# A 1-core, two-block network: the attention scores of the first block computed in two row groups at once

## The reference, cut to what matters

```python
# differential attention, 4 heads, two score maps c of 32 columns each
s = jnp.einsum('bqhcd,bkhcd->bhcqk', qi, k) * scale
p = jax.nn.softmax(jnp.where(causal, s, NEG_INF), axis=-1)
a = p[:, :, 0] - lam * p[:, :, 1]
# forgetting attention, 4 heads of 64 columns, cum = running sum of log forget gates
s = jnp.einsum('bqhd,bkhd->bhqk', qi, k) * scale
s = s + ci[..., None] - cum_k[:, :, None, :]
p = jax.nn.softmax(jnp.where(causal, s, NEG_INF), axis=-1)
```

## Time and profile before

| what | us |
|---|---|
| median of 3 runs | 2278.82 |
| lowest, highest | 2277.07, 2280.07 |
| profiled execution: its own time | 2276.64 |
| its span (first to last instruction) | 2274.9 |
| PE busy | 2214.5 (97%) |
| DVE busy | 1584.6 (70%) |
| mean granted TensorE clock | 0.983 |

### The profile page before, as it was taken

The page is one execution under the profiler, slowest core; times in us unless marked ns, Lnnn a source line. Parts: engine busy times, 40 slices in busy tenths (PEclk is TensorE's granted clock), DMA queues, the critical chain, the costliest instruction groups (busy, mean ns, idle before and its releaser), DMA issues.

```text
span 2274.9 us, 31866 instructions
## 1 busy us (share of the span) xinstructions
PE 2214.5 (97%) x11823; PEld 1866.6 (82%) x11833; DVE 1584.6 (70%) x1890; ACT 1096.2 (48%) x1288; POOL 51.3 (2%) x90
## 2 busy tenths in 40 slices
PE   7999999999999999999999999999999999999998
PEld 6887887887787887888788799978878879998887
DVE  6886877886777688666655778665566557867555
ACT  4434555434444455444544465654454446565443
POOL 1000010000000001000000000000000000000000
PEclk8999999999999999999999999999999999999999
DMA  8986555985687456666555463465556555435653
GB/s 309 348 307 208 166 170 181 343 308 187 235 293 242 144 167 204 216 220 210 176 194 183 153 183 112 149 198 184 190 167 203 185 185 150 141 114 173 201 186 109
DMA packets 325042, 454.56 MB, mean 200 GB/s; under 512 B 32722, under 2 KB 270040, under 8 KB 324952
## 3 DMA queue, kind: packets, MB, share of 16 engines
q1 hardware_dynamic: 320952, 440.98, 58.8%
q0 software_dynamic: 3728, 11.31, 1.7%
q10 hardware_dynamic: 272, 1.05, 0.1%
HBM read 449.91 MB, written 1.05 MB: 198 GB/s over the span
## 4 chain that ended last, share of the span: by engine, by line
PE 89%; DVE 6%; ACT 3%; issue 1%; DMA 1%; SPq 1%; DVEq 0%; ACTq 0%
PE ps L616 20%; PE ps L618 20%; PE ps L617 20%; PE ps L609 5%; PE ps L610 5%; PE ps L611 5%; PE ps L779 2%; PE ps L928 1%; DVE wlo L1952 1%; PE ps L761 1%; PE ps L762 1%; PE ps L764 1%; ACT whi L1329 1%; PE ps L706 1%; PE ps L727 1%
## 5 line engine op out<-in xcount | busy, mean ns | idle before, releaser
L1952 DVE TENSOR_TENSOR wlo<-raw,whi 128x2048 fp32r<-128x2048 f32 x348 | 791.5, 2278 | 364.8 <-ACT whi L1329 363.6
L1329 ACT ACTIVATE whi<-raw 128x2048 fp32r<-128x2048 f32 x346 | 659.8, 1910 | 271.4 <-PE ps L618 238.6
L616 PE MATMUL ps<-whi,xl 128*128 128x512 f32 x1472 | 591.5, 402 | 0.0
L618 PE MATMUL ps<-whi,xh 128*128 128x512 f32 x1472 | 574.2, 390 | 0.0
L617 PE MATMUL ps<-wlo,xh 128*128 128x512 f32 x1472 | 573.9, 390 | 0.0
L616 PEld LDWEIGHTS ps<-whi,xl 128*128 128x128 f32 x1472 | 276.5, 188 | 61.2 <-issue 3.8
L618 PEld LDWEIGHTS ps<-whi,xh 128*128 128x128 f32 x1472 | 276.4, 188 | 59.8
L617 PEld LDWEIGHTS ps<-wlo,xh 128*128 128x128 f32 x1472 | 276.8, 188 | 58.4 <-issue 4.3
L609 PE MATMUL ps<-xl,whi 128*128 128x256 f32 x864 | 255.2, 295 | 1.6 <-DVE wlo L1952 1.6
L616 PE MATMUL ps<-whi,hidl 128*128 128x512 f32 x640 | 252.1, 394 | 0.2 <-DVE hidl L2144 0.2
L610 PE MATMUL ps<-xh,wlo 128*128 128x256 f32 x864 | 249.4, 289 | 0.0
(11 more groups left out here) (400 smaller groups left out, 2352.9 us busy)
## 6 DMA issues: line engine op xcount, KB each, us to landing
raw<-in_ffn_w_in_dram SPq DMA_DIRECT2D x176, 512.0 KB
arena<-in_ada_w_dram SPq DMA_DIRECT2D x144, 512.0 KB, 6.1
raw<-in_w_in_dram SPq DMA_DIRECT2D x54, 1024.0 KB
raw<-in_ffn_w_out_dram SPq DMA_DIRECT2D x44, 1024.0 KB
raw<-in_w_ffn_gate_dram SPq DMA_DIRECT2D x88, 512.0 KB
raw<-in_w_ffn_up_dram SPq DMA_DIRECT2D x88, 512.0 KB
raw<-in_w_ffn_down_dram SPq DMA_DIRECT2D x44, 1024.0 KB
raw<-in_w_out_dram SPq DMA_DIRECT2D x16, 1024.0 KB
```

The lines of the kernel that those rows point to most:

```text
L616: pe.matmul(o, al, wh, start=start, stop=False, **kw)
L618: return pe.matmul(o, ah, wh, start=False, stop=stop, **kw)
L1329: act.activation(whi[:, k % 3, :], raw[:, k % 3, :], ACT.Copy).then_inc(hi_done, 1)
L1952: tt(a[0], a[1], a[2].bitcast(F32), ALU.subtract).then_inc(lo_done, 1)
```

## The change

Both groups of rows work in one stream. `paired_scores` takes the heads in pairs, one of the lower and one of the upper rows, one behind the other with no wait between, and each row group writes banks of its own: bank 3 or 4 for 256 keys, bank 2 or 5 (`PVB`) for 128 keys. The matmuls of 256 keys come first. The gate sums have a second copy of their operands in partitions 64 to 99, so that each head's gate matmul runs in the row group of its scores, right behind them and into the same open sum; the zero matmuls are gone. Since the scores now use bank 5, the fox scores wait for `gmixed`, and `convolve` waits until DVE has read the scores (`scores_read`, the third). DVE's `gate_sums` has one more copy and two half-size operations in place of one, and its setup a second clearing; POOL clears twice as many gate rows. `logits` reads the same shapes from other addresses. The second block's scores keep their order.

```diff
-            def scores(L, st, q, k, base, width, gates=False):
...
-                if gates:
-                    for b in range(3):
-                        ins = pe.matmul(ps[:, 2 + b, :], zerow[:, :], zerow[:, 0:1].to_broadcast([P, 512]), start=True, stop=True,
-                                        skip_group_check=True)
-                    st(ins)
-                last = None
-                for r0 in sorted({base(h)[0] for h in range(4)}):
-                    if last is not None:
-                        st(last)
...
-                if gates:
-
-                    st(last)
-                    for h in range(4):
-                        for qb in range(2):
-                            o, keys = out_of[qb](h), P * (qb + 1)
-                            last = pe.matmul(o, cum_left[0:GATEROWS, qb * P:qb * P + P], cum_right[0:GATEROWS, h, 0:keys],
-                                             start=False, stop=True, skip_group_check=True)
-                last.then_inc(s["scores"], 1)
+            def paired_scores(q, k, first_row, width, gates=False):
+
+                for qb in (1, 0):
+                    for c in range(2):
+                        for part in range(1 + gates):
+                            for g in range(2):
+                                r0 = 64 * g + (0 if part else first_row)
+                                rows, tok, keys = slice(r0, r0 + (GATEROWS if part else width)), slice(qb * P, qb * P + P), P * (qb + 1)
+                                left = cum_left[rows, tok] if part else q[rows, c, tok]
+                                right = cum_right[rows, 2 * c + g, 0:keys] if part else k[rows, c, 0:keys]
+                                ins = pe.matmul(paired(2 * c + g, qb), left, right, start=(part == 0), stop=(part == gates))
+                ins.then_inc(s["scores"], 1)
...
+        def paired(h, qb):
+            return (ps[:, 3 + h % 2, (h // 2) * S:(h // 2) * S + S] if qb else
+                    ps[:, (2, PVB)[h % 2], (h // 2) * P:(h // 2) * P + P])
...
-                    scores(L, st, dq, lambda r, w, ch: dk[r:r + w, ch, :],
-                           lambda h: (64 * (h % 2) + 32 * c, h // 2), 32)
+                    paired_scores(dq, dk, 32 * c, 32)
...
-                    pe.wait_ge(s["gmixed"], l + 1)
+                    pe.wait_ge(s["scores_read"], seq(L, ROUNDS, 3))
...
-                scores(L, st, fq, lambda r, w, c: fk[r:r + w, c, :], lambda h: (64 * (h % 2), h // 2), 64, True)
+                pe.wait_ge(s["gmixed"], l + 1)
+                paired_scores(fq, fk, 0, 64, True)
...
-                    stt(cum_right[32:36, :, :], cum_left[0:4, :].unsqueeze(1).to_broadcast([4, 4, S]), -1.0,
-                        ident[0:4, 0:4].unsqueeze(2).to_broadcast([4, 4, S]), ALU.mult,
-                        ALU.mult).then_inc(s["foxcum"], 1)
+                    dve.tensor_copy(cum_left[64:68, :], cum_left[0:4, :])
+                    for g, r in enumerate(GATEHALVES):
+                        ins = stt(cum_right[r + 32:r + 36, g:4:2, :], cum_left[0:4, :].unsqueeze(1).to_broadcast([4, 2, S]), -1.0,
+                                  ident[0:4, g:4:2].unsqueeze(2).to_broadcast([4, 2, S]), ALU.mult, ALU.mult)
+                    ins.then_inc(s["foxcum"], 1)
```

## The result

| | before | changed |
|---|---|---|
| median (5 runs each) | 2278.38 us | 2266.50 us |
| lowest, highest | 2277.07, 2280.07 | 2264.48, 2267.53 |
| ratio | | 0.9939, 95% interval 0.9926 to 0.9951 |
| profiled execution | 2276.64 (span 2274.9) | 2264.48 (span 2262.4) |

The changed kernel is faster by 11.9 us by the medians; the forecast was 16.6 us and 2262, with a range of 2254 to 2273. The ratio is worked out over all runs; the quotient of the two medians alone is 0.9948 and lies inside the interval. The profiled execution of the changed kernel is the fastest of its five, 2.0 us under their median.

What follows compares the result with a forecast made beforehand. TensorE (PE) bounds the kernel, with 97% of the span and 89% of the chain. Rounds (1.8, 1.0, 3.6) and clock (3.6) shorten its list by 10.0 us; waits leave 8.3 a layer, 16.6 in both: 2262 us, range 2254 to 2273.

Steps and rivals of the forecast that it cites:

- the load bound: Score rounds: weight loads don't overlap one another, 0.107 to 0.115 us each; 2.1 us per differential round, 3.8 for fox.
- the lower bound: Score rounds: two row groups fully at once, 1.28 us of array work in a differential round; rounds 1.7 and 3.0 us.
- PE's own gain: PE's list alone in a layer: 10.0 us shorter, and 1.6 us more by the skill's rule for packed row tiles.
- Falls of the clock of the old length: Sign of being wrong: in the windows of the rounds, the clock's falls to 1.2 GHz last as long as before.
- The new wait of 0.6 us: At `attend(0)`: PE 5.4 us earlier, DVE's `foxqk` only 4.8, so 0.6 us goes into waiting.
- the cap: Ahead of `convolve`: the DMAs land 328.3 to 329.4, moved by 4.8 us; start 7.7 to 8.8 us earlier, not 9.4.
- Behind it DVE and ACT follow PE: After `project(0)`: the other engines keep PE's lead, so 8.3 us in a layer, 16.6 in both, lasts to the end.
- The clock falls as often as before: Rival, mixer rounds: side by side works but clock falls stay; 6.4 us in a layer, 2266 us; chance 0.17.
- The groups take turns: Rival, score rounds: no overlap, only stops and zeros go, clock falls stay; 5.4 us off, 2273 us; chance 0.10.
- The slower case: Rival, score rounds: each row group change costs 0.46 us, 10.8 us more in a layer, 2300 us; chance 0.05.
- the likeliest case: Whole kernel: rounds overlap up to their loads, most clock loss returns, DMAs limit the gain; 2258 to 2266 us; chance 0.62.
- harder caps: Rival: fox scores or `convolve` wait 2 to 3 us more and the clock falls behind; 4 off, 2271; chance 0.06.

Runs made afterwards that it cites:

- serial rounds: Changed kernel with all matmuls of the lower rows first, then all of the upper rows, without stops or zeros: 2266.47 us, ratio 0.9942.
- the fill: Changed kernel with 7 bf16 matmuls of zeros put in PE's wait ahead of the first differential round: 2268.85 us, ratio 0.9949.
- the second profile: Changed kernel run again with no edit, in a second set of runs: median 2268.21 us, ratio 0.9947; profiled execution 2265.08 us.
- the earlier input: Changed kernel with DVE's `conv_input` ahead of `tiles(7, 8)` and `mixed_gate`, and ACT's sigmoid copy ahead of `turned_out`: 2272.44 us, ratio 0.9969.

## Why the prediction was right, and where its sum was off

**The direction and the stage.** Right: the whole gain is in the two mixer stages, and up to `convolve` it is 8.15 and 7.52 us, where 8.3 in each were forecast. That the 8.3 came out so nearly is in part luck, as the pieces of layer 0 show (read from the earlier trace rows and the rows above, a wait inside its piece):

| us, layer 0 | before | changed | difference | forecast |
|---|---|---|---|---|
| first round | 3.90 | 2.45 | -1.45 | -1.8 |
| to the second round | 8.22 | 8.37 | +0.15 | -0.9 |
| second round | 3.13 | 1.51 | -1.62 | -1.0 |
| to the fox round | 25.38 | 23.66 | -1.72 | -1.1 |
| fox round | 7.36 | 3.12 | -4.24 | -3.6 |
| to `convolve` | 9.31 | 10.04 | +0.73 | +0.1 |
| sum | 57.30 | 49.15 | -8.15 | -8.3 |

The rounds and the absence of a wait gave more than forecast, the first fall of the clock and the DMAs less, and these misses nearly cancel.

**The rounds.** The second and the fox round came out shorter than the sum had them: 1.5 us for 2.1, and 3.1 for 3.8. The first has 1.8 us of work for 2.1, but DVE's low part of the next unit, which the sum didn't have, holds PE until 2.45. The step that failed was "I take the load bound": loads of two row groups run at once, 55 ns apart, so the lower bound was the true one. The rule of the Trainium skill that stood beside it ("TensorE: Matmul & The Clock Gate", Part 3) gave the better figure, 1.7 and 3.0. By it PE's own gain was to be 1.6 us larger in a layer, and the trace agrees for the work of the rounds: 0.3, 0.6 and 0.7 us less than the sum had. The total doesn't show it, since PE waits for DVE and for the DMAs, and even serial rounds give the same total.

**The clock.** Of 8.5 us lost in a layer I let 3.4 remain, half of the first round's and half of the fox round's. Measured: all of the first round's (3.3 us), none of the fox round's, none of the second's, and in some executions a new one of 1.7 around the wait ahead of `convolve`. The sum of the old falls was right by luck; the new one wasn't in it. "Falls of the clock of the old length" was among the prediction's own signs of being wrong, and the first round's is one. Its reason for the falls, that a sparser or longer round brings them, fails for the other two: the serial rounds without stops had none behind the second and the fox round. That PE's wait ahead of the first round takes part in its fall is shown by the fill.

**What is late next.** `foxqk` was done at 308.97, 3.8 us earlier, and the first round began 0.6 later in this profile: 4.4 us for the 4.8 of the sum. The new wait of 0.6 us for it at `attend(0)` didn't come. The wait there is the old one, for ACT's copy of the turned probabilities, before and after:

```profile
313.92 0.66 PE L954 MATMUL ps<-sq,arena 128*64 128x256 f32 x4 [0.56 <-ACT sq L1574]
...
310.12 0.66 PE L950 MATMUL ps<-sq,arena 128*64 128x256 f32 x4 [0.56 <-ACT sq L1570]
```

With the first fall whole PE isn't 5.4 us early there, and `foxqk` is ready over 1 us before `attend(0)` starts. Where the fill took that fall away, PE did wait for `foxqk`, 1.0 us: the mechanism was right, its condition wasn't met. `gmixed` and `scores_read` cost nothing, as forecast. The DMAs are the cap, as forecast, and bind harder than the 1.1 us of wait that the sum held: 2.2 and 2.9 us. Between the fox round and `convolve` PE has one more new wait, 0.72 us for DVE's low part, and it hides behind the DMAs.

**The term that was mis-sized** is "Behind it DVE and ACT follow PE. I take 8.3 us in a layer, 16.6 in both." Behind `convolve` 1.60 and 1.43 us were given back: in layer 0 with a fall of the clock around PE's wait (1.7 us; the second profile of the same kernel has none there and 39.67 us, as before), in layer 1 with the new wait of 1.2 us for a modulation sum whose own weights landed late. Of the 16.6 us, 0.9 were missing at `convolve` and 3.0 were given back behind it, which leaves 12.6; 12.5 were measured between the two spans, 11.9 between the medians.

**The rivals.** "The clock falls as often as before" had 2266, just the time measured, and is out all the same by the windows: two of the three falls are gone, so its number was hit by luck. "The groups take turns" is out by the rounds. The slower case (a price for each change of row group) is out too: the second round with its 7 changes is 1.51 - 1.28 = 0.23 us over perfect overlap, the fox round with its 15, without the wait for ACT, some 2.9 - 2.56 = 0.3, so a change costs 0.03 us at most and by the difference of the two about 0.01, where 0.09 would have decided. The time, 2266.5, is just above the 2258 to 2266 of the likeliest case; what happened lies between the forecast and "harder caps".

**Still open.** How much of the gain is the stops' and how much the falls' of the clock: each version that drops the stops drops those falls too. What the DMAs are worth by themselves, since executions differ in their falls by several us (those of the changed kernel spread by 3.1 and 4.6 us in the two sets, those with the earlier input by 7.7). And why more of those are long.

## What to carry to other kernels

A stall inside a sparse stretch of PE can cost twice, as here: its own length, and the half clock that may follow it; so take out the stops first, and only then ask for parallel tiles. Before a stage is shortened, look up which transfer the next stage waits for and what runs beside it on the DMA engines: these landed some 3 to 4 us before `convolve` needed them, so they had that much cover and no more, and moving them or their neighbour only moved the wait. And look at who else shares the stage: the first round stays at 2.45 us, however short its matmuls, while DVE's low part comes when it does.

## What the runs showed of the hardware that wasn't expected

Weight loads of 128 columns in plain float32 go by every 55 ns when two row groups alternate, though alone they were 0.115 us apart. The second differential round was followed by a fall of the clock to 1.2 GHz that cost 1.7 us, the fox round by one that cost 3.4, in each of the 6 profiled rounds of either kind with stops in them, and by none in the 22 of either kind without, even when serial. The 16 DMAs from and to SBUF land 3.2, 4.5, 5.4 or 7.4 us after their issue in the median, by when they start and what weight loads run beside them. And seven matmuls of zeros in a wait of 1.6 us kept the clock at 1.00 behind the first round in four rounds of four, where 0.41 x 8 us were lost without them; in the same runs the clock fell at PE's next long wait.
